# Recurrent decay levels issued inside the gate projections, and the recurrent output and its norm moved ahead of the first branch

## What is computed

```python
G = jnp.cumsum(gc, axis=2)
diff = G[:, :, :, None, :] - G[:, :, None, :, :]
decay = jnp.exp(jnp.where(tri[:, :, None], diff, -jnp.inf))
attn = jnp.einsum('bhtd,bhsd,bhtsd->bhts', qc, kc, decay)
o = attn @ ic + jnp.einsum('bhtd,bhdv->bhtv', qc * jnp.exp(G), state)
...
y_hgrn = _rmsnorm(o, hgrn_norm_g) * jax.nn.silu(hg)
y_conv = cb * _short_conv(cc * ch, conv_w)
g = jax.nn.sigmoid(gates.reshape(b, s, N_BRANCH, D_MODEL))
mixed = (g[:, :, 0] * (y_attn @ w_up_attn)
         + g[:, :, 1] * (y_hgrn @ w_up_hgrn)
         + g[:, :, 2] * (y_conv @ w_up_conv))
x = x + mixed @ w_out
```

## Time and profile before

| what | value |
|---|---|
| runs of the kernel before | 1228.53, 1230.63, 1231.63 us; median 1230.63 |
| the profiled execution | 1233.31 us, span 1231.6 us |
| granted TensorE clock over the span | 0.98 of 2.4 GHz |
| TensorE (PE) busy | 1151.2 us, 93% of the span |
| VectorE (DVE) / ScalarE (ACT) / GpSimd (POOL) busy | 621.0 / 453.2 / 219.3 us |
| mean DMA rate | 261 GB/s |

### The profile page before, as it was taken

How to read it: one execution, slowest core, us unless ns; L and a number is a source line. 1 busy time by engine, 2 the same in 40 slices (tenths; PEclk the granted TensorE clock), 3 DMA queues, 4 the chain that set the end, 5 groups by cost and what they waited for, 6 DMA issues and landing times.

```text
span 1231.6 us, 16394 instructions
## 1 busy us (share of the span) xinstructions
PE 1151.2 (93%) x6664; PEld 809.8 (66%) x6664; DVE 621.0 (50%) x886; ACT 453.2 (37%) x702; POOL 219.3 (18%) x194
## 2 busy tenths in 40 slices
PE   7898999999888998999999888999999888999998
PEld 6866644444337886644444335889887766998996
DVE  3786711212125767711211126775599884645544
ACT  3334411111023475411111014385565534434442
POOL 5500000000011000000000000387798641000000
PEclk9998899999999999899999999999999999999999
DMA  9478599999997534799999994353353331463550
GB/s 318 131 245 351 204 397 423 422 421 421 421 389 232 183 137 185 296 397 422 421 421 420 422 369 171 138 178 109 134 189 143 137 137 69 164 246 138 199 211 35
DMA packets 86597, 321.58 MB, mean 261 GB/s; under 512 B 7128, under 2 KB 18821, under 8 KB 61947
## 3 DMA queue, kind: packets, MB, share of 16 engines
q1 hardware_dynamic: 83776, 313.08, 65.7%
q0 software_dynamic: 2192, 7.23, 1.8%
q10 hardware_dynamic: 554, 0.22, 0.1%
HBM read 318.55 MB, written 1.96 MB: 260 GB/s over the span
## 4 chain that ended last, share of the span: by engine, by line
PE 62%; DVE 17%; DMA 9%; ACT 6%; issue 2%; POOL 2%; SPq 1%; DVEq 0%; ACTq 0%
PE bank L1626 31%; PE bank L1810 20%; DMA arena<-in_moe_w_up_dram 4%; DVE w_lo L698 2%; DMA ring<-in_w_kv_dram 2%; DMA arena<-in_moe_w_down_dram 2%; ACT w_hi L1056 2%; POOL w_lo L698 2%; PE bank L1706 1%; PE bank L1879 1%; SPq L806 1%; PE bank L1843 1%; DVE arena L3030 1%; PE bank L1586 1%; PE bank L1801 1%
## 5 line engine op out<-in xcount | busy, mean ns | idle before, releaser
L698 POOL TENSOR_TENSOR w_lo<-ring,w_hi 128x512 fp32r<-128x512 f32 (+1 forms) x124 | 177.9, 1467 | 677.5 <-ACT w_hi L1056 677.5
L1056 ACT ACTIVATE w_hi<-ring 128x2048 fp32r<-128x2048 f32 (+1 forms) x102 | 191.9, 1884 | 200.3 <-PE bank L1626 198.7
L698 DVE TENSOR_TENSOR w_lo<-ring,w_hi 128x2048 fp32r<-128x2048 f32 x71 | 161.8, 2282 | 145.2 <-ACT w_hi L1056 145.1
L1626 PE MATMUL bank<-x_hi,w_hi 128*128 128x256 f32 x680 | 112.5, 288 | 2.8 <-issue 2.8
L1626 PE MATMUL bank<-x_hi,w_lo 128*128 128x256 f32 x680 | 109.8, 284 | 5.0 <-DVE w_lo L698 3.6
L1626 PE MATMUL bank<-x_lo,w_hi 128*128 128x256 f32 x680 | 109.3, 283 | 0.8 <-DVE x_lo L2367 0.7
L1810 PE MATMUL bank<-arena 128*64 128x512 f32 x352 | 98.6, 594 | 2.3 <-ACT arena L1056 1.5
L1626 PE MATMUL bank<-w_hi,x_hi 128*128 128x512 f32 x320 | 93.2, 406 | 7.4 <-DVE x_lo L2490 3.0
L1626 PEld LDWEIGHTS bank<-x_hi,w_lo 128*128 128x128 f32 x680 | 93.5, 191 | 5.8 <-DVE w_lo L698 4.0
L1626 PEld LDWEIGHTS bank<-x_hi,w_hi 128*128 128x128 f32 x680 | 93.4, 191 | 5.6 <-issue 5.1
L2668 DVE TENSOR_TENSOR y_r<-bank,y_r 128x512 fp32r<-128x512 f32 x32 | 22.1, 692 | 144.6 <-ACT y_r L1056 144.6
(11 more groups left out here) (357 smaller groups left out, 1625.9 us busy)
## 6 DMA issues: line engine op xcount, KB each, us to landing
ring<-in_w_in_dram SPq DMA_DIRECT2D x15, 2048.0 KB, 7.8
arena<-in_moe_w_gate_dram SPq DMA_DIRECT2D x24, 1024.0 KB, 15.5
ring<-in_moe_w_gate_dram SPq DMA_DIRECT2D x24, 1024.0 KB, 15.8
arena<-in_moe_w_down_dram SPq DMA_DIRECT2D x24, 1024.0 KB, 21.5
ring<-in_moe_w_down_dram SPq DMA_DIRECT2D x24, 1024.0 KB, 18.8
ring<-in_moe_w_up_dram SPq DMA_DIRECT2D x24, 1024.0 KB, 19.9
arena<-in_moe_w_up_dram SPq DMA_DIRECT2D x24, 1024.0 KB, 22.6
wslots<-in_moe_w_up_dram SPq DMA_DIRECT2D x16, 1024.0 KB, 17.7
```

What stands on the lines that cost most here:

```text
L698: last = ops.tensor_tensor(part(w_lo, label, hb)[:, x].bitcast(F32R), ring_half(label, hb)[:, x], part(w_hi, label, hb)[:, x], ALU.subtract)
L1056: return s.activation(dst, src, ACT.Copy)
L1626: last = mm(bank(use_)[0:still.shape[1], at:at + cols], still, moving, start=start and opens and (hb, n, k) == (0, 0, 0), stop=stop and cl ...
```

## The change

`LEVEL_AT` gives for each of the eight levels the half block (two to a block, counted from the start of `hg`) ahead of whose first tile it is issued on TensorE: levels 0 to 7 at half blocks 0, 2, 3, 5, 6, 8, 9, 11, in place of 0, 2, 4, 6, 8, 10, 12, 14. `DECAY_AT` does the same for the exponentials on ScalarE; an even number stands ahead of `high(coming, 0)`, an odd one behind it. `lev01` moves ahead of the second half of block 6, and the recurrent output ahead of that half's second tile. On VectorE the split of the attention's rows and the `w_lo` of that branch move behind the sums of squares, and both parts of `hgrn_norm` ahead of the first `gated`. The transposes `yhT` move from unit 2 of the second half of the convolution branch to unit 2 of the first. On ScalarE the first `high` of the convolution branch moves behind the two square roots. No instruction is added or removed.

```diff
@@ -71,6 +71,8 @@
 BIAS_SPAN = P + T - 1
 
 BRANCHES = (0, 2, 1)
+LEVEL_AT = (0, 2, 3, 5, 6, 8, 9, 11)
+DECAY_AT = (1, 2, 4, 5, 7, 8, 10, 12)
 BETWEEN = {0: ("hg",), 1: ("gates", 0), 2: ("gates", 1), 3: ("gates", 2), 4: ("gates", 3), 5: ("gates", 4),
            6: ("gates", 5)}
 
@@ -1491,13 +1493,21 @@
             high("hg", 1)
             channels_out("cb", cb, 1)
 
-            for n in range(len(LEVELS) + 1):
-                act.wait_ge(sem("hdiff"), n + 1)
-                s.activation(ez, ez, ACT.Exp).then_inc(sem("hdecay"), 1)
-                coming = ("gates", n) if n < 6 else ("branch", BRANCHES[0]) if n == 6 else None
-                if coming:
-                    high(coming, 0)
-                for t in range(NT if n in BETWEEN else 0):
+            def decays(half):
+                for m in range(len(LEVELS) + 1):
+                    if DECAY_AT[m] == half:
+                        act.wait_ge(sem("hdiff"), m + 1)
+                        s.activation(ez, ez, ACT.Exp).then_inc(sem("hdecay"), 1)
+
+            for n in range(len(LEVELS)):
+                coming = ("gates", n) if n < 6 else ("branch", BRANCHES[0])
+                decays(2 * n)
+                high(coming, 0)
+                decays(2 * n + 1)
+                if n == len(LEVELS) - 1:
+                    ready(act, "lev01")
+                    free(copy(att01, bank("lev01")[:].rearrange("p (h t) -> p h t", h=HH)), "lev01")
+                for t in range(NT):
                     use_ = (*BETWEEN[n], t)
                     ready(act, use_)
                     if n == 0:
@@ -1507,21 +1517,17 @@
                 if n == len(LEVELS) - 1:
                     freed(act, ("yaT", 1))
                     copy(x_hi[:, 0:4, :].bitcast(F32R), yaT).then_inc(sem("ya_hi"), 1)
-                if coming:
-                    high(coming, 1)
+                high(coming, 1)
                 if n == 0:
                     ready(act, ("yaT", 0))
                     free(copy(yaT[:, 0:2, :], bank(("yaT", 0))[:].rearrange("p (c t) -> p c t", c=2)), ("yaT", 0))
-            ready(act, "lev01")
-            free(copy(att01, bank("lev01")[:].rearrange("p (h t) -> p h t", h=HH)), "lev01")
             act.wait_ge(sem("yc"), 1)
             copy(x_hi[:, 4:8, :].bitcast(F32R), ycT).then_inc(sem("yc_hi"), 1)
             for t in range(NT):
-                if t == 0:
-                    high(("branch", 2), 0)
                 act.wait_ge(sem("hms"), t + 1)
                 s.activation(hstd[:, t, :], hms[:, t, :], ACT.Sqrt, scale=1.0 / VD, bias=eps_rms[:])\
                  .then_inc(sem("hstd"), 1)
+            high(("branch", 2), 0)
             high(("branch", 2), 1)
             high(("branch", 1), 0)
             for b in range(2):
@@ -2251,7 +2257,8 @@
             channels("cb", steps=during_cb)
             weighted2(7)
 
-            for n in range(len(LEVELS) + 1):
+            def level(n):
+
...
@@ -2260,32 +2267,44 @@
                         last = mm(bank(("lev", n, t))[:, h * P:(h + 1) * P], k_[:, h, t * P:(t + 1) * P],
                                   q_[:, h, t * P:(t + 1) * P], start=True, stop=True)
                     full(last, ("lev", n, t))
-                if n in BETWEEN:
-                    linear_tok(BETWEEN[n], BETWEEN[n] if len(BETWEEN[n]) > 1 else BETWEEN[n][0])
-                if n == 0:
+
+            def recurrent_out(t):
+                claim(pe, ("oh", t))
+                pe.wait_ge(sem("att"), t + 1)
+                if t:
+                    freed(pe, "lev01")
+                for h in range(HH):
+                    o = bank(("oh", t))[:, h * P:(h + 1) * P]
+                    if t:
+                        mm(o, att01[:, h, :], itok[:, 0, h * P:(h + 1) * P], start=True, stop=False)
+                    last = mm(o, attT[:, t, h, :], itok[:, t, h * P:(h + 1) * P], start=t == 0, stop=True)
+                full(last, ("oh", t))
+
+            def during_gates(i):
+
+                def steps(hb, t):
+                    if t == 0:
+                        for n in range(len(LEVELS) + 1):
+                            if LEVEL_AT[n] == 2 * i + hb:
+                                level(n)
+                    if i == len(LEVELS) - 1 and (hb, t) == (1, 0):
+                        claim(pe, "lev01")
+                        pe.wait_ge(sem("hqk"), len(LEVELS) + 2)
+                        for h in range(HH):
+                            last = mm(bank("lev01")[:, h * P:(h + 1) * P], ke[:, h, 0:P], qe[:, h, P:T], start=True, stop=True)
+                        full(last, "lev01")
+                    elif i == len(LEVELS) - 1 and (hb, t) == (1, 1):
+                        for t_ in range(NT):
+                            recurrent_out(t_)
+                return steps
+
+            for i in range(len(LEVELS)):
+                linear_tok(BETWEEN[i], BETWEEN[i] if len(BETWEEN[i]) > 1 else BETWEEN[i][0], steps=during_gates(i))
+                if i == 0:
                     for qt in range(NT):
                         freed(pe, ("o2", qt))
                     for b in range(2):
                         pieces(("yaT", b), [lambda t, c=2 * b + j: yat[:, t, c * P:(c + 1) * P] for j in range(2)])
-            def recurrent_out(hb, n):
-                if (hb, n) != (1, 0):
-                    return
-                claim(pe, "lev01")
-                pe.wait_ge(sem("hqk"), len(LEVELS) + 2)
-                for h in range(HH):
-                    last = mm(bank("lev01")[:, h * P:(h + 1) * P], ke[:, h, 0:P], qe[:, h, P:T], start=True, stop=True)
-                full(last, "lev01")
-                for t in range(NT):
-                    claim(pe, ("oh", t))
-                    pe.wait_ge(sem("att"), t + 1)
-                    if t:
-                        freed(pe, "lev01")
-                    for h in range(HH):
-                        o = bank(("oh", t))[:, h * P:(h + 1) * P]
-                        if t:
-                            mm(o, att01[:, h, :], itok[:, 0, h * P:(h + 1) * P], start=True, stop=False)
-                        last = mm(o, attT[:, t, h, :], itok[:, t, h * P:(h + 1) * P], start=t == 0, stop=True)
-                    full(last, ("oh", t))
             for b in range(2):
                 freed(pe, ("yaT", b))
 
@@ -2295,12 +2314,12 @@
                               steps=steps, order=order)
 
             def recurrent(hb, n):
-                if (hb, n) == (1, 2):
+                if (hb, n) == (0, 2):
                     pe.wait_ge(sem("yh"), NT)
                     for b in range(2):
                         pieces(("yhT", b), [lambda t, c=2 * b + j: yh[:, t, c * P:(c + 1) * P] for j in range(2)])
             pe.wait_ge(sem("ya_lo"), 1)
-            branch(0, slice(0, 4), recurrent_out)
+            branch(0, slice(0, 4))
             pe.wait_ge(sem("yc_lo"), 1)
             branch(2, slice(4, 8), recurrent)
             for b in range(2):
@@ -3064,12 +3083,9 @@
                     ready(dve, ("yaT", 1))
                     free(v.tensor_copy(yaT[:, 2:4, :], bank(("yaT", 1))[:].rearrange("p (c t) -> p c t", c=2)), ("yaT", 1))
                 short_conv(n)
-            dve.wait_ge(sem("ya_hi"), 1)
-            v.tensor_tensor(x_lo[:, 0:4, :].bitcast(F32R), yaT, x_hi[:, 0:4, :], ALU.subtract).then_inc(sem("ya_lo"), 1)
             ready(dve, ("lev", len(LEVELS), NT - 1))
             decayed(len(LEVELS) + 1, T)
             masked_in(len(LEVELS))
-            low(dve, v, ("branch", BRANCHES[0]), 1)
             for t in range(NT):
                 ready(dve, ("oh", t))
                 free(v.tensor_copy(yh[:, t, :], bank(("oh", t))[:]), ("oh", t))
@@ -3086,6 +3102,11 @@
                 link(v.tensor_tensor(y, y, bcast(hng[:].unsqueeze(1), HH, VD), ALU.mult))
                 freed(dve, ("hg", t))
                 v.tensor_tensor(yh[:, t, :], yh[:, t, :], hgs[:, t, :], ALU.mult).then_inc(sem("yh"), 1)
+            dve.wait_ge(sem("ya_hi"), 1)
+            v.tensor_tensor(x_lo[:, 0:4, :].bitcast(F32R), yaT, x_hi[:, 0:4, :], ALU.subtract).then_inc(sem("ya_lo"), 1)
+            low(dve, v, ("branch", BRANCHES[0]), 1)
+            for t in range(NT):
+                hgrn_norm(t)
 
             def gated(br, t):
                 for h in range(2):
@@ -3105,10 +3126,8 @@
             dve.wait_ge(sem("yc_hi"), 1)
             v.tensor_tensor(x_lo[:, 4:8, :].bitcast(F32R), ycT, x_hi[:, 4:8, :], ALU.subtract).then_inc(sem("yc_lo"), 1)
             gated(0, 0)
-            hgrn_norm(0)
             low(dve, v, ("branch", 2), 1)
             gated(0, 1)
-            hgrn_norm(1)
             for b in range(2):
                 dve.wait_ge(sem("yh_hi"), b + 1)
                 free(v.tensor_tensor(x_lo[:, 2 * b:2 * b + 2, :].bitcast(F32R),
```

## The result

The kernel got slower. Its median is **1256.79 us** (four runs, 1252.92 to 1260.57), that of the kernel before beside it 1229.58 us (1227.11 to 1231.63): a ratio of **1.0208 [1.0183, 1.0233]**, 27.2 us. The forecast was 1248 us in a range of 1239 to 1258, and slower with a chance of 0.88. The sign and the mechanism of the levels held; of the size, a third was missed.

The account below looks back on a forecast made before the run. The prediction took VectorE's rounds, 14.07 us and lengthened by POOL's blocking, to set the pace. Level losses of 22.8 less 5.5 recovered gave +17.3; with +0.8 and −0.5 for the branches, +17.6 us: 1248 us, range 1239 to 1258.

Parts of the forecast that it names:

- What bounds the kernel: In the gates, VectorE's round of 14.07 us against TensorE's 12.7 sets the pace; free of POOL it would be 7.8.
- The levels' losses: TensorE's waits at levels 2 to 7 and lev01, for late factors and masks: 22.8 us in sum.
- The masks: At a level where TensorE already waits for factors, it also waits for VectorE's masks of the level before: 1.7 us.
- The late exponential: At levels 3, 7 and lev01 the exponential stands behind ScalarE's evacuation and rounding: TensorE waits 1.6 us each.
- The clock: TensorE's falls to half speed: no term in the sum, only a rival at 1252 to 1255 us, chance 0.10.
- The branches: Behind the gates: attention branch +0.8 us for ya_lo, convolution branch net −0.5, recurrent output the same 3.6 in its new place.
- The sum: Levels +17.3 us, attention branch +0.8 and convolution branch −0.5 make +17.6 us, giving 1248 us.
- VectorE gets free: Rival: TensorE's waits leave POOL idle, its blocks vanish and rounds at levels 3 to 6 shorten: 1222 us, chance 0.07.
- The losses cancel: Rival: early roundings meet the late exponentials, rounds fall to some 10 us: within 3.7 us of 1230.6, chance 0.05.
- The clock falls as well: Rival: waits as at levels 4 and 6 bring two to four half-speed falls of 1.8 us: 1252 to 1255, chance 0.10.
- levels as worked out: The main case: the levels lose what the sum along TensorE gives, +17.6 us in all, chance 0.78.

Follow-up runs that it names:

- e8_no_pool_before: The kernel before, with POOL making only 16 columns of each w_lo half of the gates (most of the subtraction left out): 1226.16 us, ratio 0.9957.
- e4_fill: The changed kernel with matmuls nobody reads ahead of TensorE's wait for factors at levels 2, 3, 4, 6 and 7: 1251.99 us, ratio 1.0167.
- e9_conv_early: The kernel before with the first three operations of the short convolution moved ahead of `heads2_out(1)` on VectorE: 1229.03 us, ratio 0.9981.
- e7_no_pool: The changed kernel, with POOL making only 16 columns of each w_lo half of the gates (most of the subtraction left out): 1234.94 us, ratio 1.0035.

## Why the prediction came out as it did

**What bounds the kernel.** Right. VectorE's round, doubled by POOL, is the pace that the denser levels run into. The 7.8 us forecast for a round free of POOL was 7.95, and the experiment without POOL's work took away two thirds of the loss.

**The levels' losses.** 22.8 forecast, 25.6 measured. Level 2 was met (3.4 for 3.3); level 4 was taken too high (2.9 for 4.7), the others too low. In the done times: level 7 was forecast done at 965.1 − 868.85 = 96.25 us after level 0, and was done at 964.45 − 864.49 = 99.96, 3.7 later, of which 0.8 is half speed at level 7 itself and 1.2 that of the gate products behind level 6. The step that was loose is the round after each late exponential, taken at 11.9 to 14.07. The levels 3 to 7 started 11.3, 14.7, 11.7 and 19.1 us apart: short where level 4's factors followed early, long at level 7, since a late level also makes ScalarE's evacuations late, and the next exponential with them. I had let each level start from the last one's factors, and not carried the lateness through ScalarE.

**The masks.** The mechanism is in the trace (waits of 0.23 to 0.58 us ahead of the second tiles of five levels), but 1.7 us a level was not its price: with other banks most of the same time is waited for factors. What it does cost is open, since those banks brought a wait of 2.9 us of their own.

**The late exponential.** 4.8 us forecast (1.6 at three levels); moving the exponentials was worth 10.4. Too low, for the reason given.

**The clock.** The step that failed. The sum had no term for it; it stood as a rival with a chance of 0.10 and "two to four of them" at 1.8 us. There were five stretches at half speed, four of 3.4 us and one of 6.8. Against it I had put that one wait of 2.8 us left the clock alone. One such row proves nothing: in e8_no_pool_before the same wait for the norm is followed by half speed for 3.4 us (1.05 us for a pair of products in place of 0.62). The timeline of PE, e8_no_pool_before:

```profile
986.89 1.09 PE L2136 MATMUL bank<-ident,res 128*128 128x128 f32 x8 [2.83 <-DVE res L3100]
...
988.33 1.05 PE L1638 MATMUL bank<-w_hi,x_lo 128*128 128x512 f32 x2
```

What the levels bring is waits of 1.3 to 3.4 us, again and again, and e4_fill shows that these waits are what brings most of the half speed; why one of them does and the next doesn't, no run shows. The price in the end is 5.8 us by the trace: 4.6 from level 7 on and the 1.2 behind level 6. Half speed at level 3 is hidden in a wait.

**The branches.** 0.8 for `ya_lo` was 1.2; the convolution branch −0.5 was −1.6 (0.37 for `w_lo` instead of 1.3; bank 3 1.43 instead of 1.8; the norm and `yc_lo` as said). The recurrent branch's `w_lo` now comes from POOL 1.29 us late, 1.0 that I had not seen. Together 0.6 for 0.3.

**The sum.** 17.6 forecast, 25.4 in the stretch. The difference of 7.8 is 3.7 up to level 7 done, 0.6 of half speed behind it, 0.5 at lev01, 1.7 + 1.5 of half speed behind that, and 0.3 in the branches; that is 8.3, half a microsecond too much. That 1256.79 still lies within the range is in part luck: the upper end of 1257 was worked out from multiplications that are all blocked, and of the pairs at the late exponentials one was blocked and one free, as in the sum.

**The rivals.** *VectorE gets free* didn't happen: POOL idled 74.0 us in waits for ScalarE, as that rival wanted, yet VectorE's operations were still blocked (a multiplication of 1.75 us at 901.76), and without its work two thirds of the loss go. Its pauses didn't lie where VectorE worked, but for one round (from 911.05 to 920.83, 9.8 us). *The losses cancel* neither. *The clock falls as well* came on top of the levels as worked out, and its time, up to 1256, was the nearest.

## What to carry to other kernels

Work that a chain feeds (here exponential, multiplications, matmul, mask) can on average be issued no closer together than the chain's round, and that round is to be measured where it will run, under contention: 14.07 us here, and 7.95 by itself. When a queue is made denser, look at the places in the other in-order queues too: moving three exponentials by half a block was worth 10.4 us, the pair of norms 2.8. And waits of a few microseconds on TensorE that come again and again have a second price, half speed for work behind them: it counts where no wait follows, and also where the next wait is for something that these products release.

## What the runs showed of the hardware

- In the changed kernel TensorE was at half speed for 20.5 us of the stretch: behind the waits of 2.59, 3.36 and 2.59 us ahead of levels 3, 6 and 7, behind that of 1.99 ahead of lev01, and in the attention branch behind 3.12. Behind those of 2.33, 2.13 and 1.27 ahead of levels 2, 4 and 5 it wasn't. With products to no purpose in the waits it was 6.8 us (e4_fill). In the changed kernel the gate products ahead of level 3 had run without a gap for 11 us when the wait came, and the level behind it ran at half speed all the same.
- The same wait can go either way. That for the norm, 2.82 or 2.83 us, had half speed behind it in e8_no_pool_before, and none in the kernel before and in e9_conv_early; the 3.12 us ahead of the attention branch had it in the changed kernel, and none in e7_no_pool, where TensorE kept full speed throughout the stretch.
- In a stretch in which VectorE and POOL were busy 83% and 88% of the time, a round of VectorE took 14.07 us; with most of POOL's subtractions left out it took 7.95.
- The load of ScalarE's function table costs its 1.28 us and nothing ahead of it: in the ACT fence around 896 us it starts 0.02 us after the rounding's end (896.76 + 1.91), and the exponential 0.01 after its own.
